# Gate and up of an expert split by output columns over TensorE's four column groups, in place of a split by halves of the contraction

## What is computed

```python
def hmoe(v, w_rg, b_rg, w_re, b_re, w_gate, w_up, w_down):
    ...
    def expert_block(args):
        xb, e = args
        hb = jax.nn.silu(xb @ w_gate[e]) * (xb @ w_up[e])
        return hb @ w_down[e]
    ...
    ys = (ypad[dest] * gw_s[:, None]).astype(v.dtype)
    return jnp.zeros((T, D), v.dtype).at[tok_s].add(ys)
```

## Time and profile before

| | before |
|---|---|
| time, median of 3 runs | 1733.64 us (1729.73 to 1734.1) |
| time of the profiled execution | 1736.11 us |
| its span | 1734.5 us |
| mean granted TensorE clock | 0.936 of full speed |
| TensorE matmul busy | 88% of the span |
| VectorE, ScalarE busy | 55%, 33% |
| HBM traffic over the span | 213 GB/s |

### The profile page before, as it was taken

One profiled execution on the slowest core, in us unless ns is written; L12 is line 12 of the kernel. 1 busy time (PEld: TensorE's weight loads), 2 busy tenths in 40 slices (PEclk: granted clock), 3 DMA queues, 4 the chain that ended last, 5 costly groups with the idle time before them and its releaser, 6 DMA issues.

```text
span 1734.5 us, 32723 instructions
## 1 busy us (share of the span) xinstructions
PE 1528.4 (88%) x11355; PEld 1078.1 (62%) x11355; DVE 957.2 (55%) x1693; ACT 577.0 (33%) x849; POOL 303.0 (17%) x316
## 2 busy tenths in 40 slices
PE   4899999889999959999928999999989999977772
PEld 4788989878889947858825454544445555533330
DVE  6655547579988969766664323133423223234349
ACT  4322314255566555212201333133323233233210
POOL 4000012100000010000002323223322323322200
PEclk9999999989999979999958999999999999988886
DMA  9666136443334356223296849358984838789742
GB/s 295 203 242 210 51 95 227 139 119 118 111 121 139 111 205 218 85 88 100 73 376 250 318 172 367 126 193 320 389 352 163 330 149 335 314 328 412 299 185 111
DMA packets 157310, 366.02 MB, mean 211 GB/s; under 512 B 16040, under 2 KB 94944, under 8 KB 149944
## 3 DMA queue, kind: packets, MB, share of 16 engines
q1 hardware_dynamic: 138184, 308.19, 48.4%
q0 software_dynamic: 18480, 54.80, 9.0%
q10 hardware_dynamic: 576, 2.10, 0.4%
HBM read 324.15 MB, written 45.73 MB: 213 GB/s over the span
## 4 chain that ended last, share of the span: by engine, by line
PE 44%; DVE 5%; DMA 5%; ACT 4%; issue 2%; SPq 2%; DVEq 1%; ACTq 0%; POOLq 0%
PE PS L2091 15%; PE PS L1967 9%; PE PS L2100 9%; PE PS L2110 6%; DMA ring<-in_w_down_dram 4%; ACT ring L1910 3%; PE PS L2146 1%; PE PS L2080 1%; DVE ring L2451 1%; PE PS L1998 1%; PE PS L2033 1%; ACT lower L1890 1%; SPq L1601 1%; PE PS L1990 1%; DVE st L2505 0%
## 5 line engine op out<-in xcount | busy, mean ns | idle before, releaser
L886 PE MATMUL PS<-big 128*128 128x352 f32 x2592 | 436.5, 328 | 1.7 <-DVE big L1140 1.7
L886 PEld LDWEIGHTS PS<-big 128*128 128x128 f32 x2592 | 425.0, 191 | 10.4 <-issue 6.7
L2091 PE MATMUL PS<-ring,arena 128*32 128x512 f32 x2624 | 326.2, 642 | 0.5 <-DVE arena L2408 0.5
L2100 PE MATMUL PS<-pick,lower 128*128 128x64 f32 x656 | 171.1, 407 | 53.6 <-ACT lower L1890 53.6
L2100 PEld LDWEIGHTS PS<-pick,lower 128*128 128x128 f32 x656 | 159.3, 327 | 89.0 <-ACT lower L1890 68.0
L2091 PEld LDWEIGHTS PS<-ring,arena 128*32 128x32 f32 x2624 | 81.6, 117 | 176.8 <-issue 157.8
L1747 POOL DMA_INDIRECT lower<-v_d,icur x84 | 100.3, 1194 | 459.9 <-DVE icur L2420 319.1
L1910 ACT ACTIVATE ring<-ring 128x1024 f32 x124 | 121.2, 1046 | 129.0 <-PE PS L2091 79.7
L2110 PE MATMUL PS<-ring,lower 128*32 128x256 f32 x2624 | 158.6, 382 | 1.0 <-DVE lower L2416 1.0
L2441 DVE COPY ring<-ring 128x1024 f32 x124 | 78.0, 689 | 101.3 <-PE PS L2091 52.0
L1755 POOL DMA_INDIRECT f_d<-lower,scur x82 | 121.7, 1484 | 61.0 <-issue 50.0
(11 more groups left out here) (427 smaller groups left out, 1873.2 us busy)
## 6 DMA issues: line engine op xcount, KB each, us to landing
ring<-in_w_gate_dram SPq DMA_DIRECT2D x32, 2048.0 KB, 7.6
ring<-in_w_up_dram SPq DMA_DIRECT2D x32, 2048.0 KB, 12.3
ring<-in_w_down_dram SPq DMA_DIRECT2D x32, 2048.0 KB, 18.2
arena<-in_w_ada_dram SPq DMA_DIRECT2D x16, 1024.0 KB, 6.7
arena<-in_w_in_dram SPq DMA_DIRECT2D x20, 512.0 KB, 8.0
upper<-in_w_ada_dram SPq DMA_DIRECT2D x8, 1024.0 KB, 12.0
upper<-in_w_in_dram SPq DMA_DIRECT2D x16, 512.0 KB, 3.8
arena<-acs_d SPq DMA_DIRECT2D x8, 1024.0 KB, 4.8
```

The lines of the kernel that those rows point to most:

```text
L886: mm = pe.matmul(PS[:, 3 * b + a, 0:CH], wss[b][:, i, k, :], us[:, j, k, a * CH:(a + 1) * CH], start=(k == 0 and (i, j) == PARTS[0]), stop ...
L2091: mm = pe.matmul(PS[32 * g:32 * g + 32, 3, :], xT[:, c, CAP * q:CAP * q + CAP], wcur[:, 4096 * part + 1024 * q + 512 * c:4096 * part + 102 ...
L2100: mm = pe.matmul(PS[:, 4, 2 * CAP * c:2 * CAP * c + 2 * CAP], hb[:, c::FF // P], pick[:, :, :].rearrange("p m r -> p (m r)"), start=True, ...
```

## The change

Three layouts change together.

1. `gate_up`: before, column group g multiplied one half of the contraction (the features of parity c, as `xT[:, c]`) with all 512 columns of gate or up, so that bank 3 held two partial sums of gate and two of up, 512 columns wide. Now a group multiplies both halves, one after the other, with 256 columns of gate or up. Bank 3 holds finished sums, 256 columns wide.
2. `h_turn`: before, four matmuls with every fourth column of `hb` as the stationary operand and the constant `pick` as the moving one turned `hb` and added the two partial sums. Now two plain transposes of 128 contiguous columns do. `pick` is gone, and `hb_out` copies 256 columns.
3. Hidden value 128c + p now lies on partition p, where it was 4p + c before. So the down weights are loaded as `(c p) n -> p c n`: four rows of 4 KB for a partition that lie apart in memory, in place of one piece of 16 KB. `down` reads its 32 stationary columns at another place of `hT`.

```diff
                 def load_down(x):
                     s = SLOTS - x % SLOTS if x else 0
-                    sp.dma_start(ring[:, SLOT * s + 8192:SLOT * s + 12288],
-                                 w_down[0, x].rearrange("(p c) n -> p (c n)", p=P)).then_inc(we_loaded[s], 16)
+                    sp.dma_start(ring[:, SLOT * s + 8192:SLOT * s + 12288].rearrange("p (c n) -> p c n", c=FF // P),
+                                 w_down[0, x].rearrange("(c p) n -> p c n", p=P)).then_inc(we_loaded[s], 16)
...
-                    act.activation(hb, PS[:, 3, :], ACT.Copy).then_inc(hb_ready, 1)
+                    act.activation(hb, PS[:, 3, 0:FH], ACT.Copy).then_inc(hb_ready, 1)
...
-                        for g in range(4):
-                            part, c = g // 2, g % 2
-                            mm = pe.matmul(PS[32 * g:32 * g + 32, 3, :], xT[:, c, CAP * q:CAP * q + CAP],
-                                           wcur[:, 4096 * part + 1024 * q + 512 * c:4096 * part + 1024 * q + 512 * c + FF],
-                                           start=(q == 0), stop=(q == QW - 1))
+                        for c in range(2):
+                            for g in range(4):
+                                w = 4096 * (g // 2) + 1024 * q + 512 * c + FH * (g % 2)
+                                mm = pe.matmul(PS[32 * g:32 * g + 32, 3, 0:FH], xT[:, c, CAP * q:CAP * q + CAP],
+                                               wcur[:, w:w + FH], start=(q == 0 and c == 0),
+                                               stop=(q == QW - 1 and c == 1))
                         mm.then_inc(gu_mm, 1)
...
-                    for c in range(FF // P):
-                        mm = pe.matmul(PS[:, 4, 2 * CAP * c:2 * CAP * c + 2 * CAP], hb[:, c::FF // P],
-                                       pick[:, :, :].rearrange("p m r -> p (m r)"), start=True, stop=True)
+                    for c in range(2):
+                        mm = pe.transpose(PS[:, 4, P * c:P * c + P], hb[:, P * c:P * c + P], ident[:, :])
                     mm.then_inc(hT_mm, 1)
...
-                            mm = pe.matmul(PS[32 * g:32 * g + 32, 6, 0:DQ], hT[:, c, :],
+                            mm = pe.matmul(PS[32 * g:32 * g + 32, 6, 0:DQ], hT[:, c % 2, CAP * (c // 2):CAP * (c // 2) + CAP],
```

More of the change, by code:

```diff
@@ L1394, in build_step @@
         rowidx = sb("rowidx", [P, P])
-        pick = sb("pick", [P, 2, CAP])
         slot_step = sb("slot_step", [P, NE])
@@ L1450, in build_step @@
         yo = [at3(R1 + 512 + DQ * b, DQ) for b in range(2)]
-        hb, xT = at3(R1 + 1024, FF), at2(11264, 2, P)
-        hT, hth, h1 = [at3(R1 + 1536 + 128 * i, FF // P, CAP) for i in range(3)]
-        idxT, idxS = [at3(R1 + 1920 + NBLK * i, NBLK).bitcast(I32) for i in range(2)]
-        ctl = at3(R1 + 1920 + 2 * NBLK, 3 * NBLK + 2 * NE + 1).bitcast(I32)
+        FH = FF // 2
+        hb, xT = at3(R1 + 1024, FH), at2(11264, 2, P)
+        hT, hth, h1 = [at3(R1 + 1280 + 128 * i, 2, 2 * CAP) for i in range(3)]
+        idxT, idxS = [at3(R1 + 1664 + NBLK * i, NBLK).bitcast(I32) for i in range(2)]
+        ctl = at3(R1 + 1664 + 2 * NBLK, 3 * NBLK + 2 * NE + 1).bitcast(I32)
         gate2, ln2g, ln2b = [at2(7168 + D * i, D) for i in range(3)]
@@ L1702, in _ @@
                 step(gp.memset(slot_step[:, 0::2], -float(SLOT)))
-                four = ident[:, :].rearrange("p (m j r) -> p m j r", m=2, j=2)
-                step(gp.tensor_tensor(pick[:, :, :], four[:, :, 0, :], four[:, :, 1, :], ALU.add))
                 gp.tensor_copy(lane[:, 0:1], lane_int[:, 0:1]).then_inc(gpsimd_once, 1)
@@ L1882, in _ @@
                 act.activation(gsm[:, 4, :], gsm[:, 4, :], ACT.Exp).then_inc(scalar_once, 1)
-                half = PS[:, 4, 0:2 * CAP * (FF // P)].rearrange("p (c m r) -> p c m r", m=2, r=CAP)
+                half = PS[:, 4, 0:2 * P].rearrange("p (c m r) -> p c m r", c=2, m=2)
                 def hb_out(u):
```

## The result

| | before | after |
|---|---|---|
| time, median of the runs | 1732.49 us (4 runs, 1729.73 to 1734.1) | 1632.93 us (4 runs, 1631.13 to 1638.7) |
| after / before, 95% interval | | 0.9433 (0.9404 to 0.9462) |
| time of the profiled execution | 1736.11 us | 1638.7 us |
| its span | 1734.5 us | 1636.9 us |
| first to last h_turn | 720.1 us | 620.8 us |

The change takes 99.6 us off. The forecast was 1620, with a range of 1602 to 1660. All of the gain stands between the first and the last h_turn; what lies behind the last h_turn is 1.4 us shorter. The first h_turn came at 936.3 instead of 933.2 us, and over all profiled executions of this study it came between 929.5 and 937.4 in no relation to the edit, so those 3 us are nothing of the change's.

What follows compares the result with a forecast made beforehand. TensorE was taken to set the pace of plain periods, h_turn being a quarter. Terms -79.6, -30.1, 0, +3.9, -7 and -1.8 sum to -114.6 us: 1736.1 to 1621.5, by the runs' median 1619, stated as 1620, range 1602 to 1660.

Steps and rivals of the forecast that it cites:

- 51 plain periods: Periods without a gate copy, set by TensorE's four steps: 7.88 to 6.32 us each, 79.6 us saved in all.
- the clock's -7: Half-clock gate_up steps after switches and waits: 4 fewer of 12, 7 us saved, between -20 and +20.
- 17 plain switches: Periods with gate copies, set by ScalarE's path: 8.90 to 7.13 us, 1.77 less each, 30.1 us saved.
- 7 double switches: Periods where VectorE's list takes over: TensorE waits for x_out before gate_up, period stays near 8.6 us, gain 0.
- 6 waits for weights: Periods bound by memory's full stream: savings given back and smaller down pieces cost +3.9 us, with up to +15.
- ends and start of the stage: Outside the 81 periods: the last h_turn and a shorter first hb_out save 1.8 us.
- h_turn's 0.44: New h_turn to the next step's start, priced from x_turn: 0.44 us in place of 2.01, 1.57 saved.
- the rival by which longer gate_ups make the kernel slower: In gate_up, TensorE runs out of queued instructions, rounds take 0.35 us in place of 0.214: 1760 us; chance 0.02.
- the rule cited in the prediction: About 62 ns of sequencer time per MATMUL: gate_up an estimated 3.97 us, 25 to 32 us lost; judged not to bind.
- The rival that all 24 switches would be followed by one: Transposes don't count as clock activity, so each switch brings a half-clock stretch of 1.70 us: 1646 us; chance 0.08.
- Elsewhere it is covered: Outside full stretches the slower down load costs nothing: an expert needs 15.8 us of stream and lasts about 19.2.
- more than ten would make it wrong: Sign of failure in the experts' stage: more than ten periods waiting for weights, where six or a few more were expected.

Runs made afterwards that it cites:

- b_turn: The kernel before with only the new h_turn, two contiguous transposes that leave half of the values unturned; 1631.02 us, ratio 0.9402.
- b_split: The kernel before with only gate_up's new order, 64 matmuls of 256 columns in place of 32 of 512; 1733.16 us, ratio 1.0006.
- b_contig: The kernel before with h_turn's four matmuls reading contiguous columns of hb in place of every fourth; 1656.20 us, ratio 0.9545.
- a_signal: The changed kernel with a separate landing signal for the down load, so gate copies don't wait for it; 1624.55 us, ratio 0.9378.
- a_down16k: The changed kernel with the down weights loaded in 16 KB pieces, as before the change; 1631.17 us, ratio 0.9412.
- a_light: The changed kernel with gate and up loaded by half from expert 3 on, 4.2 MB an expert in place of 6.3; 1616.47 us, ratio 0.9320.

## Why the prediction was right, and where its sum was off

The forecast was a saving of 114.6 us against the profiled execution; it saved 97.4 (99.6 between the medians). By the prediction's own terms (periods sorted as before; a half-clock step is inside the class in which it falls):

| term | forecast, us | measured, us |
|---|---|---|
| 51 plain periods, with the clock's -7 | -86.6 | -83.8 (418.2 to 334.4) |
| 17 plain switches | -30.1 | -17.3 (151.1 to 133.8) |
| 7 double switches | 0 | -4.2 (60.5 to 56.3) |
| 6 waits for weights | +3.9 | +6.0 (90.3 to 96.3) |
| ends and start of the stage | -1.8 | +1.7 |

**The mechanism held.** TensorE sets the pace of plain periods, h_turn is the step that shrinks, gate_up doesn't grow. h_turn's 0.44 was 0.37; the price was taken from x_turn, whose weight loads read every second column (mean 207 ns) while h_turn's are contiguous (145). b_turn and b_split show each half by itself, -103 us and nothing, and the rival by which longer gate_ups make the kernel slower is gone with them. The double switches were the mechanism's second half, and the size there was right in part by luck (below).

**The instruction rate.** 64 matmuls in 3.59 us are 56 ns each, in the change and in b_split. That leaves the rule cited in the prediction without effect here: by the roughly 62 ns a MATMUL that the Trainium skill, "TensorE: Matmul & The Clock Gate" (Wait — 56ns, not 53.3ns?), gives for a sequencer without hardware decode, the step would have been an estimated 3.97 us, and the trace is 0.38 below it.

**The clock.** Gate_up steps of 5.0 to 5.7 us fell from 12 to 7. That band, which is the prediction's, leaves out some steps on both sides. Counted by the granted clock the half-clock steps went from 16 to 13, three fewer where four were forecast, and their cost from 27.7 (the prediction had 20.4) to 22.5 us: 5.2 less in place of 7. Seven of the 13 stand right behind the seven double switches; before, none did. The rival that all 24 switches would be followed by one did not come. In the calm window above, with two pairs of transposes in each unit, the granted clock was 1.00 for 31 us. The Trainium skill, "TensorE: Matmul & The Clock Gate", Part 4 (transposes don't count as activity) thus made no visible difference there. Whether they count stays open: b_turn, whose h_turn is two transposes in 0.37 us, has 14 half-clock steps, and b_contig, with eight matmul instructions in 1.03 us, has 8.

**The mis-sized term: the plain switches.** It is -17.3 in place of -30.1. Three of the 17 lasted 10.3, 11.3 and 10.4 us in place of about 7.1, which is 10.7 us of the 12.8 by which the term is short. Two steps of the prediction failed in these three.

- The larger part is the wait behind a double switch. TensorE waited 1.5, 1.7 and 1.9 us for x_out there, and gate_up then took 5.0, 5.3 and 5.3 us at the half clock. The prediction had this wait, but inside the double switch, and a half-clock step behind it only as something that might come.
- The smaller part is "Elsewhere it is covered", by which the stream of weights would cost nothing outside the six old waits. In a_signal, where no gate copy waits for SyncE in these three periods, they still last 8.8, 9.2 and 9.9 us. So 4.0 of the 10.7 us goes with the weights, and 6.7 stays without them.

**The waits that were not forecast.** With the three in double switches 12 gate copies wait, where the prediction had said that more than ten would make it wrong: on the count it was wrong, though the time stayed inside its range. The six new ones cost 10.1 us, 4.0 in the switches and 6.0 in the double switches, by the same periods in a_signal. The mean over all experts (19.2 us against 15.8 of stream) hid that short experts stand in a row, and that the word for a landed expert comes later than its gate and up.

**The cause of the waits.** The prediction put the six old waits down to the stream. The runs show two bounds close together, the stream and the loop of signals (tables above), so the waits' +3.9 was near for a reason that was only half right.

**The double switches** were forecast as no gain, by a wait of TensorE for x_out. That wait came, but in the period behind the double switch: five times, 7.0 us, of which 5.1 lie in plain switches. The four double switches without a wait for weights lasted 7.3, 7.1, 7.3 and 6.8 us in place of the forecast 8.6, and the other three 10.0, 9.6 and 8.3. So the class gained 4.2 where 0 was forecast, since a gain and new waits that the term didn't have nearly cancel: the size was near by luck, and the place was off by one period.

**A term that the sum put at nothing: pauses inside gate_up.** The prediction took 3.58 us for every gate_up and named over 3.8 as a sign that it is wrong. A plain step took 3.59, but 17 of the 82 took 3.9 to 4.4 us at the full clock, where the kernel before had none. Over 3.59 each they sum to 9.2 us, 5.5 in plain periods and 3.8 in plain switches. The wider gain of h_turn (0.07 x 51 = 3.6) hides part of it. This is the largest single piece of the 13.5 us by which the stage gained less than forecast (112.8 against 99.3).

## What to carry to other kernels

When the stationary operand of a transposing matmul is read at a stride, look at its weight loads first: here contiguous columns alone brought a kernel 78 us, where the whole change brought 100. When the engine that sets the pace gets faster, reread what each signal really stands for: one word for three loads cost about 5 us before the change and 8 after it. When a list of one engine makes another wait, look for the cost in the period behind as well: the wait for x_out fell there, and with it a gate_up at the half clock. In this kernel changes of order were worth nothing, or less, by themselves: hb_out first gained nothing, x_out first lost some 9 us, and the two together with split signals gained 12 over the split signals alone.

## What the runs showed that was not expected

The weight load of 128 float32 columns took 329 ns at a stride of four words, 192 ns contiguous (b_contig), in the same four matmuls with the same moving operand. Nothing in the prediction had a price for a stride.

In the 17 longer gate_up steps of the change TensorE pauses inside the step, for no semaphore that the profile shows. The timeline of TensorE around one, first a normal step and then the longer one:

```profile
970.56 3.66 PE L2090 MATMUL PS<-ring,arena 128*32 128x256 f32 x64
...
976.82 4.33 PE L2090 MATMUL PS<-ring,arena 128*32 128x256 f32 x64
```

Its weight loads show where, after 38 of 64, and that nothing was waited for:

```profile
976.82 1.88 PEld L2090 LDWEIGHTS PS<-ring,arena 128*32 128x32 f32 x38 [0.17 <-issue]
979.24 1.43 PEld L2090 LDWEIGHTS PS<-ring,arena 128*32 128x32 f32 x26 [0.54 <-issue]
```

The granted clock is 1.00 there. In nine others a gap of 0.41 to 0.61 us stands after 39 to 51 weight loads. The seven shortest (3.9 to 4.0 us) show no gap over 0.23, and what stretches them isn't seen. b_turn (32 wider matmuls, the short turn) and b_split (64 matmuls, the long turn) have no such step, and a_down16k has 17 too. So it takes both, many small matmuls and the short turn; the change's shorter copy of hb was not tested apart from them.

The pauses also go with the weight stream. In the change all 17 fell among the 51 full-clock steps during which the DMA engines were busy for about 80% or more, and none in the 13 with less than 25%. In a_light, with a third fewer bytes, 34 steps lie under 30%, and the only pause among them is in the last step of the stage, behind the loop. What the transfers could hold up in TensorE's sequencer stays open; no run here was made for it.
